# More early places for expert parts, filled in the order in which they come free

## The reference, cut to what matters

```python
h = h + short_conv_mixer(...)      # layer 0
h = h + hier_moe(rmsnorm_2(h, g), w_grp, w_exp, w_gate, w_up, w_down)
h = h + mla_mixer(...)             # layer 1: attention over a shared latent
h = h + hier_moe(...)
return rmsnorm_2(h, final_norm_g)

def expert_block(xb, e):           # for the tokens of expert e
    hh = silu(xb @ w_gate[e]) * (xb @ w_up[e])      # 1024 -> 256
    return hh @ w_down[e]                           # 256 -> 1024
```

## Time and profile before

| | |
|---|---|
| Median of three runs | 2392.33 us (2390.03 to 2392.79) |
| Profiled execution, time | 2391.24 us |
| Profiled execution, span | 2389.4 us |
| PE busy | 2200.7 us (92%) |
| DVE busy | 1083.6 us (45%) |
| ACT busy | 382.6 us (16%) |
| DMA, mean over the span | 259 GB/s |
| Mean granted clock of PE | 0.97 |

### The profile page before, as it was taken

One profiled execution on the slowest core, in us unless ns is written; L12 is line 12 of the kernel. 1 busy time (PEld: TensorE's weight loads), 2 busy tenths in 40 slices (PEclk: granted clock), 3 DMA queues, 4 the chain that ended last, 5 costly groups with the idle time before them and its releaser, 6 DMA issues.

```text
span 2389.4 us, 28251 instructions
## 1 busy us (share of the span) xinstructions
PE 2200.7 (92%) x10664; PEld 1319.8 (55%) x10664; DVE 1083.6 (45%) x2079; ACT 382.6 (16%) x911; POOL 56.3 (2%) x95
## 2 busy tenths in 40 slices
PE   8999999999999999999999999898899987777776
PEld 7865558854885556884585444343347533322222
DVE  6665646654766665666322433333333243222222
ACT  1212231103210232110301100000022310000001
POOL 3000000000100000000000000000000000000000
PEclk9999999999999999999999999999999999888888
DMA  9542435433852343632662899999992399999997
GB/s 331 200 164 88 159 124 176 177 110 129 266 208 109 141 141 106 211 145 92 194 236 106 335 421 422 422 422 422 422 409 94 128 407 418 422 422 422 422 421 319
DMA packets 209293, 619.16 MB, mean 259 GB/s; under 512 B 15229, under 2 KB 120518, under 8 KB 161078
## 3 DMA queue, kind: packets, MB, share of 16 engines
q1 hardware_dynamic: 202144, 610.25, 66.1%
q0 software_dynamic: 1600, 5.06, 0.6%
q10 hardware_dynamic: 5462, 2.67, 0.4%
HBM read 616.89 MB, written 1.05 MB: 259 GB/s over the span
## 4 chain that ended last, share of the span: by engine, by line
PE 68%; DMA 24%; SPq 2%; issue 2%; DVE 2%; ACT 1%; DVEq 0%; POOL 0%; POOLq 0%; ACTq 0%
DMA ring<-expert_parts 23%; PE PS L2637 22%; PE PS L2720 11%; PE PS L1709 7%; PE PS L1613 4%; PE PS L2824 3%; PE PS L2778 3%; PE PS L2965 2%; PE PS L1665 2%; SPq L1044 1%; PE PS L793 1%; PE PS L1193 1%; PE PS L2807 1%; PE PS L1725 1%; SPq L1101 1%
## 5 line engine op out<-in xcount | busy, mean ns | idle before, releaser
L1709 PE MATMUL PS<-ring,arena 128*32 128x512 f32 x1984 | 275.5, 707 | 136.3 <-DMA ring<-expert_parts 134.6
L2637 PE MATMUL PS<-ring,xT 128*128 128x256 f32 x1056 | 244.9, 382 | 3.5 <-ACT xT L1924 3.5
L1709 PEld LDWEIGHTS PS<-ring,arena 128*32 128x32 f32 x1984 | 67.5, 126 | 318.0 <-issue 160.8
L2637 PEld LDWEIGHTS PS<-ring,xT 128*128 128x128 f32 x1056 | 201.3, 191 | 31.6 <-ACT xT L1924 4.2
L1665 PE MATMUL PS<-arena,xn 128*128 128x128 f32 x1280 | 203.4, 297 | 12.5 <-DVE h L1518 12.3
L1665 PEld LDWEIGHTS PS<-arena,xn 128*128 128x128 f32 x1280 | 163.9, 189 | 72.9 <-issue 30.0
L1525 DVE TENSOR_TENSOR arena<-PS,arena 128x512 f32<-128x512 f32 x64 | 44.3, 692 | 270.7 <-PE PS L1665 270.7
L2637 PE MATMUL PS<-arena,xn 128*128 128x256 f32 x704 | 165.8, 379 | 0.0
L2720 PE MATMUL PS<-ring,arena 128*128 128x512 f32 x352 | 162.8, 592 | 0.0
L1577 DVE TENSOR_TENSOR arena<-arena,PS 128x256 f32<-128x256 f32 x30 | 12.7, 422 | 286.8 <-ACT arena L1321 286.8
L2637 PEld LDWEIGHTS PS<-arena,xn 128*128 128x128 f32 x704 | 130.6, 190 | 16.1
(11 more groups left out here) (421 smaller groups left out, 2712.1 us busy)
## 6 DMA issues: line engine op xcount, KB each, us to landing
ring<-expert_parts SPq DMA_DIRECT2D x368, 1024.0 KB, 18.2
ring<-ffn_gate_up SPq DMA_DIRECT2D x88, 1024.0 KB, 10.2
ring<-ffn_down SPq DMA_DIRECT2D x44, 1024.0 KB, 7.3
ring<-w_in SPq DMA_DIRECT2D x16, 768.0 KB, 6.1
ring<-conv_w_in SPq DMA_DIRECT2D x12, 1024.0 KB, 12.7
ring<-expert_parts SPq DMA_DIRECT2D x16, 512.0 KB, 13.8
ring<-w_out_rows SPq DMA_DIRECT2D x8, 768.0 KB, 6.8
ring<-ple_gate SPq DMA_DIRECT2D x8, 768.0 KB, 5.7
```

What stands on the lines that cost most here:

```text
L1709: last = mm(PS[BLK * j:BLK * (j + 1), 2, :], lhsT=xgT[:, k, j * BLK:(j + 1) * BLK], rhs=ahead_row(j, k) if is_ahead and half == 0 else gu[ ...
L2637: last = mm(out, lhsT=a[:, k, :], rhs=b[:, 256 * k:256 * (k + 1)], start=k == 0, stop=k == 3)
```

## The change

- **Places.** `mixed_rows` packs small tiles of the first block (tables, rope, gains) into one tile whose first 1024 columns are free in the expert stages. With it and other leftovers there are spare places (`SPARE`), nearly all in pieces of 512 columns: two for stage 0, three for stage 1 (the third in tile 2 of h and of xn, which layer 1 doesn't use).
- **Order.** For groups 1 and 2 the parts have no fixed place. `homes` lists the places in the order in which PE leaves them: spares, ring low, ring high, ring down, ahead, spares. The parts (`ITEMS`, from the high parts of group 1 on) take them one after the other. Group 3 goes back to the ring, its experts' numbers still constants; the table is read from group 4 on. The loads of groups 1 and 2 signal on semaphores of their own, and the low half of group 1 waits for a count that the high parts of group 1 raise too.
- **Early.** Three quarters of a spare part load at the very start of stage 0's loads. Behind mla_uq, three down parts of stage 1's group 0, two times three quarters and a whole part of group 1 are loaded under the attention.
- **Last group.** The combination of the first output half is moved between the two halves of `down`, for all tiles but the last.
- **Final gains.** ACT loads them after the third group of stage 1.
- Warm-up matmuls read const2 instead of const; a third group is written out on PE.

```diff
-        ahead = [xT[:, :, :].rearrange("p k t -> p (k t)")[:, 0:PART], rowsf[:, 1024:1024 + PART], arena[:, 8896:8896 + PART]]
-        AHEAD_LOADS = [7, 7 + 4 + 7]
+        SPARE = [chunks_of(mixed_rows[:, 0:1024]) + [const[:, LEVELS_AT - 512:LEVELS_AT], rowsf[:, 3072:3584]],
+                 [rowsf[:, 3584:4096], arena[:, 0:512], arena[:, 5424:5936], arena[:, 6192:6704]],
+                 chunks_of(h[:, 2, :]) + chunks_of(xn[:, 2, :])]
+        SPARES = [[SPARE[0], SPARE[1]], [SPARE[2], SPARE[0], SPARE[1]]]
+        ITEMS = [(1, 1), (1, 2), (2, 0), (2, 1), (2, 2)]
+        def home(i, g, n, j):
+            if g == 0:
+                return RING[n][j]
+            if (g, n) == (1, 0):
+                return AHEAD[j]
+            homes = SPARES[i] + RING[0] + RING[1] + RING[2] + AHEAD + SPARES[i]
+            return homes[GROUP * ITEMS.index((g, n)) + j]
...
             load(3, ring[:, 3, 0:4608], A["mla_uq"], 3)
+            for j in range(GROUP - 1):
+                sp.dma_start(ring[:, j, 2 * PART:3 * PART], A["expert_parts"][1][j, 2]).then_inc(M[1].dn_loaded, 16)
+            for q in range(3):
+                first_load(sp, 1, 1, 0, 3, q)
+                first_load(sp, 1, 1, 1, 1, q)
+            sp.wait_ge(S.h2_sq, 3)
+            sp.wait_ge(S.h2_turned, H2_TURNED[2] + 5)
+            for q in range(4):
+                first_load(sp, 1, 1, 1, 0, q)
             sp.wait_ge(S.mla_down_done, 6)
...
+            if i == 0:
+                sp.wait_ge(S.pe_step, 1)
                 for j in range(GROUP):
+                    whole(1, 0, j, S_mla[4])
+                first_load(sp, 0, 1, 1, 0, 3)
+                whole(1, 1, 1, S_mla[4])
+            else:
+                for j in (1, 2):
+                    whole(1, 0, j, S_mla[4])
+                first_load(sp, 1, 1, 0, 3, 3)
+                first_load(sp, 1, 1, 1, 1, 3)
+                whole(1, 1, 2, S_mla[4])
+                sp.wait_ge(S.pe_step, 4)
+                whole(1, 0, 0, S_mla[4])
...
+            sp.wait_ge(gate_up_used[0], GROUP)
+            for at in range(spares, spares + 4):
+                item(at)
+            sp.wait_ge(gate_up_used[1], GROUP)
+            for at in range(spares + 4, spares + 8):
+                item(at)
+            sp.wait_ge(down_used, 2 * GROUP)
+            for at in range(spares + 8, spares + 12):
+                item(at)
+            sp.wait_ge(gate_up_used[0], 2 * GROUP)
+            for at in range(spares + 12, spares + 16):
+                item(at)
+            sp.wait_ge(gate_up_used[1], 2 * GROUP)
+            for at in range(spares + 16, 20):
+                item(at)
+            sp.wait_ge(down_used, 2 * 2 * GROUP)
+            for j in range(GROUP):
+                gate_up(slice(3 * GROUP + j, 3 * GROUP + j + 1), j, 0)
...
+                down(g, ns=(0,), is_last=True)
+                pe.wait_ge(M[i].added, nt * g + nt + 1)
+                pe.wait_ge(M[i].y_copied, 2 * g + 3)
+                weighted(0, range(nt - 1))
+                down(g, ns=(1,), is_last=True)
+                weighted(0, (nt - 1,))
+                pe.wait_ge(M[i].y_copied, 2 * g + 4)
+                weighted(1, range(nt))
```

More of the change, by code:

```diff
@@ L101, in const_table @@
     put("inv_freq", inv[None])
+    put("spare", np.zeros((P, 96)))
     masks = []
@@ L1050, in down, with whole @@
                 part(e, j, 2).then_inc(M[i].dn_loaded, 16)
+            def whole(g, n, j, loaded):
+                dst = {id(RING[a][c]): ring[:, c, PART * a:PART * (a + 1)] for a in range(3) for c in range(GROUP)}
+                dst.update({id(AHEAD[0]): xT[:, :, :].rearrange("p k t -> p (k t)")[:, 0:PART],
+                            id(AHEAD[1]): rowsf[:, 1024:1024 + PART], id(AHEAD[2]): arena[:, 8896:8896 + PART]})
+                space, src = home(i, g, n, j), A["expert_parts"][i][GROUP * g + j, n]
+                if id(space) in dst:
+                    sp.dma_start(dst[id(space)], src).then_inc(loaded, 16)
+                else:
+                    for q in range(4):
+                        sp.dma_start(space[q], src[:, 512 * q:512 * (q + 1)]).then_inc(loaded, 16)
+            if i == 0:
+                for q in range(3):
+                    first_load(sp, 0, 1, 1, 0, q)
             for pair in ((0, 1), (2, 3)) if i == 0 else ((2, 3), (0, 1)):
@@ L1081, in experts @@
+            for j in range(GROUP):
+                gate_up(slice(3 * GROUP + j, 3 * GROUP + j + 1), j, 0)
+            sp.wait_ge(gate_up_used[0], 3 * GROUP)
+            for j in range(GROUP):
+                gate_up(slice(3 * GROUP + j, 3 * GROUP + j + 1), j, 1)
+            sp.wait_ge(gate_up_used[1], 3 * GROUP)
+            for j in range(GROUP):
+                down(slice(3 * GROUP + j, 3 * GROUP + j + 1), j)
             sp.wait_ge(S.routed, i + 1)
@@ L1317, in moe_act, with group @@
             act.preload_act_table_set("silu_and_others")
-            with act.Fori(0, groups) as g:
+            def group(g):
                 act.wait_ge(gu_used[i][1], g * GROUP + GROUP)
@@ L1327, in moe_act @@
                     a_.activation(ysb[:, 512 * n:512 * n + 512], PS[:, 4 + n, :], ACT.Copy).then_inc(M[i].y_copied, 1)
+            with act.Fori(0, 3) as g:
+                group(g)
+            if i:
+                act.dma_start(rows[:, 3, :], A["final_norm_g_2"].unsqueeze(0).to_broadcast([P, D])).then_inc(S.final_loaded, 16)
+            with act.Fori(3, groups) as g:
+                group(g)
         def second_vec(dve, rstd):
@@ L1686, in combine @@
                 last.then_inc(M[i].combined, 1)
-            gu = [ring[:, j, 0:2 * PART].rearrange("p (k w) -> p k w", k=KD) for j in range(GROUP)]
             def hidden_turn(g):
@@ L1737, in first_group, with rest @@
                 select(2, HIGH[:1])
-                down(0)
+                down(0, 0)
                 select(2, HIGH[1:])
-            def rest(g):
+            def rest(g, static=None):
                 combine(g, 0)
```

153 lines of the change are left out of this document (85 added, 68 removed).

## The result

The kernel after takes 2378.6 us (median of 4 runs, 2377.65 to 2380.6), the kernel before on the same chip 2392.56 (4 runs, 2390.03 to 2393.46). The ratio is 0.9945, interval [0.9933, 0.9958]: 14.0 us less. The forecast was 8.1 less, 2384.2, with a range from 2380.5. So the direction was right and the gain too small, outside the range. The profiled execution took 2380.6 us with a span of 2378.8 and a mean granted clock of 0.97; the profiled executions differ by 10.6 us, the medians by more.

A forecast was written before the change was run, and what follows sets the result against it. The prediction took each expert stage, between fill and last load, to be bound by its transfers. Its terms, -4.97 - 7.46 + 2.5 + 1.25 + 0.7 - 0.1 = -8.1 us, gave 2384.2 us, range 2380.5 to 2389.5.

The forecast's parts named there:

- The places (-12.43): Both expert stages: two more places in stage 0 save 4.97 us, three more in stage 1 save 7.46.
- So +0.7 us, bounds 0 and +0.9: End of stage 0: in the new order PE waits about 1 us for ACT's copy, costing 0.7 us.
- the forecast's -0.1: End of stage 1: the new order of the last group does the same total of work, -0.1 us.
- 5 x 0.5 = +2.5: Behind the releases: five parts, each split into four 256 KB DMAs, cost 0.5 us each; bounds 1.0 and 7.5.
- The slower-than-before rival: Loaded queue: small pieces cost more than the places bring; at 4 us extra a part, 2402 us; chance 0.05.
- Between its fill and its last load each stage runs at the speed of its transfers: Both expert stages: DMA share of 1.01 at 422 and 421 GB/s, so 2.49 us for each 1 MB part.
- a release comes late: Rival, kernel after: a release 3.7 us late holds all loads behind it; stage 0's gain goes, 2389.2 us; chance 0.12.
- The gains row (+1.25): Stage 1: the 512 KB final gains load now falls amid the full stream and costs 1.25 us.
- PE closes stage 0: Rival: PE, not loads, ends stage 0; lower clock or slowed attention gives back 2 to 4 us, 2387; chance 0.12.
- No stall: Behind the first releases, both stages: loads and PE's new wait in group 1 are in time; tightest load margin 3.7 us.
- The attention (0): Between the stages: the attention stays as long as before, with 5.5 parts loaded under it; change 0.
- its best case, -11.0: Whole kernel: the favourable bounds of all terms together give 11.0 us less, 2381.3 us.

The follow-up runs named there:

- the five loads: The kernel after with the final gains loaded five times instead of once, at the same place of the stream: 2382.64 us, ratio 0.9961 to the kernel before.
- the one behind the stream: The kernel after with SP loading the final gains behind the last load of stage 1: 2377.59 us, ratio 0.9931 to the kernel before.

## Why the gain was larger than forecast, point by point

The terms for the places and for the gains row were right. Three steps failed, all to the same side: the order of the last group in stage 0 was priced as a loss (+0.7, measured -0.7), the quartered parts were priced too high (+2.5, measured +1.35), and stage 1 of the kernel before was taken for a stream without a hole, where its windows show 1.0 us of them.

**The places (-12.43): right.** Taking away two of them in stage 0 and three in stage 1 costs 7.3 and 10.4 us, which is 4.97 and 7.46 and what the quartered DMAs cost at the head of the burst; in stage 0 the windows bear out that second piece (2.1 of 2.3). The fills ended near 1326 and 1927, before the releases at 1332.22 and 1928.49. The first wait of PE came one group later in stage 0.

**"So +0.7 us, bounds 0 and +0.9" for the last group in stage 0: wrong in sign.** Measured: -0.7 (mean of two and two profiles), and -0.6 from the kernel in the old order. The step read "the second half before starts at 1774.45 with almost no wait" as if it were a fact of the schedule. It was the meeting of two times in one execution, and the row at that time, the weight load of the second half, names the last load as what released it (timeline of PEld, before):
```profile
1774.45 0.16 PEld L1725 LDWEIGHTS PS<-ring,arena 128*32 128x32 f32 x8 [0.97 <-DMA ring<-expert_parts]
```
The window behind PE's wait for group 14's high half shows why they met, first in the profile of the earlier trace rows:
```profile
1733.00:1740.00 7.00, 6.18 (x32) 1.38 (x32) 0.00 (x0) 0.00 (x0) 0.00 (x0) 0.53 1.01 423
```
then in the second profile of before:
```profile
1734.00:1741.00 7.00, 6.00 (x34) 1.75 (x35) 0.03 (x1) 0.38 (x1) 0.00 (x0) 0.76 1.01 421
```
The granted clock is 0.53 in the one, nearly all at the 1.2 GHz level, and 0.76 in the other; the 32 records take 6.46 and 5.34 us. So in the first PE came 1.1 us later in its stage, just as the last load landed. In the second profile of before and in the kernel in the old order PE waits 1.27 and 1.40 us for that load, and this is the wait that the moved combination fills.

All thirteen profiles agree on this. In the four with the old order in stage 0 the second half starts 40.6 to 40.7 us behind the start of the tail, when the last load is in, whether PE starts on down at 37.2 or at 38.6, and the tail is 48.2 to 48.4. In the nine with the new order PE doesn't wait for that load, and the tail is 10.3 us more than the time at which PE starts on down, 36.7 to 37.5: 47.0 to 47.8. By this sum a PE as late as in the earlier trace rows, at 38.6, would have had a tail of 48.9 in the new order, 0.6 more than it had. So the forecast's +0.7 was right for the one execution that it was read from and had the wrong sign for every other. The bound should have reached to a gain: the load's landing time was worth working out from the stream, 2.49 us a part, and PE's arrival at either clock beside it. In stage 1 the change of tail, -0.15, is near the forecast's -0.1; five kernels whose PE was at full clock there have 15.3, against the 16.2 of the old order, which is the 0.85 that the forecast named as its best case.

**"5 x 0.5 = +2.5" for the quartered parts: right in kind, too dear.** In the kernel after, stage 0 loses 10 x (1 - 386/422) = 0.85 us at its three such parts and stage 1 10 x (1 - 401/422) = 0.50 at its two: 1.35 in all, 0.27 each. The experiment with 30 of them gives 0.37 each. The value of 0.5 came from a window at the end of a fill, where the queue runs empty. At the head of a burst a part costs 1.0 to 1.2, and the kernel after has none there. Half of that gap is the place: moved behind four whole parts, two of them still cost 1.3 together, 0.65 each, and why they cost more than 0.27 isn't shown. The slower-than-before rival needed 3.1 a part and is excluded. The Trainium skill (DMA: Bandwidth & Descriptors, "Rules for kernel authors") asks for at least 1 MiB in a DMA. The trace agrees that smaller is slower, 388 against 422 GB/s in a full stream, but by 8% and not by the fixed cost of its fit, which that page gives for single DMAs issued by GpSimd.

**"Between its fill and its last load each stage runs at the speed of its transfers": not quite, in stage 1 of the kernel before.** I took a DMA share of 1.01 over 425 us for a stream without a hole. A hole of 1 us is 0.2% of that window. Windows of the kernel before at two places of stage 1:
```profile
1962.00:1965.00 3.00, 3.00 (x11) 1.42 (x8) 1.41 (x2) 0.38 (x1) 0.00 (x0) 1.00 0.91 344
1973.00:1976.00 3.00, 3.00 (x31) 1.96 (x33) 1.91 (x5) 0.00 (x0) 0.00 (x0) 1.00 0.97 360
```
and the timeline of SP of the kernel before at the same time:
```profile
1962.19 2.18 SPq L1044 DMA_DIRECT2D ring<-expert_parts  x4
```
The high parts of group 2 go to the places that group 1's high parts leave. PE started on these at 1955.51, behind its wait of 6.04 us, and was done at 1962.05; SP issued at 1962.19. The twelve parts in the queue from 1933.3 end at 1933.3 + 12 x 2.49 = 1963.2. A load comes into its rate some 1.6 us behind its issue (at the head of stage 0's stream, issued at 1332.39, the us from 1333 has 115 GB/s and the next 295), so here at 1963.8. So the release came late, in the kernel before and not after. It came late because PE had the lower clock behind its wait: these 32 records took 6.54 us, where 3.64 would have released at 1959.2. The window in the kernel before:
```profile
1955.00:1961.00 6.00, 5.49 (x28) 1.58 (x32) 0.00 (x0) 0.00 (x0) 0.00 (x0) 0.50 1.01 422
```
The two windows of the dips lose 3 x (1 - 344/422) = 0.55 and 3 x (1 - 360/422) = 0.44 us, 1.0 together. The second dip stands where group 2's down parts begin; SP issued them at 1971.42, which by the same sum isn't late, so its cause is open. The second profile of before has the first dip again at nearly the same distance from the start of the stage, behind 5.93 us for the same records: its window
```profile
1966.00:1968.00 2.00, 2.00 (x6) 0.87 (x5) 1.10 (x2) 0.00 (x0) 0.00 (x0) 1.00 0.85 258
```
loses 0.8 (a second, shallow one, 391 GB/s from 1976 to 1979, another 0.2). With the new order these loads go to places that were left earlier, whatever the number of spares. The kernel whose stage 1 has its spares behind the release runs through that stretch, as its windows show.
```profile
1957.00:1960.00 3.00, 3.00 (x29) 1.43 (x22) 0.00 (x0) 1.20 (x2) 0.00 (x0) 1.00 1.01 421
1961.00:1969.00 8.00, 4.99 (x45) 2.29 (x43) 3.71 (x12) 0.00 (x0) 0.00 (x0) 0.99 1.01 422
```
No experiment changed the order of the places alone, so the microsecond is read from the traces and isn't isolated. The rival "a release comes late" was looked for in the wrong kernel.

**The gains row (+1.25): right.** It is 1.27 by the five loads, 1.2 by the one behind the stream. What the forecast didn't see is that behind the last load it gives nothing for certain either.

**"PE closes stage 0" (the rival at 2387): no.** Tail 0 got no longer, and the time saved in stream 0 arrived at the end. The forecast's row for it was misread, though: from 1733.82 to the end of the last weighted sum it is 48.3 us and not some 42, and in the old order the last load is waited for inside it. It is with the new order that PE, and no load, closes the stage. "No stall" behind the releases held as well: the dips of the stream after the release are at the quartered parts. PE's new wait inside the last down was there, 0.79 us.

**The attention (0): right.** It takes 145.8 or 147.5 us, in kernels with and without the early loads, and before and after. The 1.7 us is PE at the lower clock for a stretch: eight of the thirteen profiles have about 147.5, each with a granted clock under 1 between 1840 and 1860, and five have 145.8, with 1.00 there. The window of the kernel after has it:
```profile
1839.00:1846.00 7.00, 5.07 (x20) 4.10 (x18) 3.46 (x10) 1.54 (x6) 0.00 (x0) 0.76 0.00 0
```
The second profile of before has the like at 1842 to 1852, granted 0.83 in the mean, and its attention is 147.5 too.

**The sum again, with what was measured:** -12.43 + 1.35 (quartered parts) + 1.27 (gains) - 0.85 (last group, both stages) - 1.0 (holes of the stream in before) = -11.7, against -12.15 between the mean spans. Of the 3.6 us between this and the forecast, 1.15 is the price of the quartered parts, 1.45 the last group, 1.0 the holes. Some 0.5 us isn't accounted for. The medians differ by 14.0 and 13.0, one to two more than the profiles: the profiled execution of before was 1.1 us under the median that the forecast had, that of after 2.0 over its own, and runs of one kernel spread by 3 us (after) and by 3 to 11 us (before, in its four sets), in which a lower clock in the attention is 1.7. Where the rest of the spread comes from isn't shown. The range was wrong by its best case, -11.0, which held no gain in tail 0 and no hole in the stream before. That the median came 1.9 us below the range, more than these two steps explain by the profiles, is in part chance: the forecast was anchored to one profiled execution.

## What to carry to other kernels

In a stage bound by its transfers, count the bytes that are in before the stream becomes continuous: here each 1 MB place more was worth about 2.49 us, to within a tenth or two in stage 0, provided that it was filled in idle time. Look for holes of a microsecond with windows of a few microseconds around each release, in the kernel before too, since a share of 1.01 over a whole stage hides them and a new order of places can remove them. And where PE arrives within a few microseconds of a load, don't price the meeting from one profile: work out both arrival times, with PE at either clock, and let the bounds take in both signs.

## What was unexpected of the hardware

- DMAs of 256 KB with rows of 2 KB move 388 GB/s in a full queue, but 248 to 293 in the first 8 us behind an idle stretch, where DMAs of 1 MB with rows of 8 KB move 420. Behind four whole parts a run of eight of them still starts with a dip, 287 GB/s over 4 us. Why the start of such a run is slow stays open: SP issues one in about 0.5 us, and one moves in 0.62 us at 422 GB/s, so the issue alone is not late.
- Two executions of one kernel differ by 1.7 us in the attention, where nothing but the granted clock of PE differs: 0.76 in a 7 us window of one of them.
- 5.5 parts of 1 MB written into the core under the attention, most of them, at 276 GB/s over 16 us, made PE's work there no longer.
